# Where an arena in SBUF begins: 32 instead of 64 bytes beyond a multiple of 128

## The reference, cut to what matters

```
h = rms_norm(x);  proj = h @ w_in
x = x + merged(attention, rwkv, short conv; gates) @ w_out
x = x + square(relu(rms_norm(x) @ w_up)) @ w_down
```

```
u = causal_dwconv(h @ ffn_w_up);  y = (silu(gate) * val) @ ffn_w_down
x = layer_norm(DN_ALPHA * x + (1 + gate2) * y)
```

## Time and profile before

| | |
|---|---|
| median of 3 runs | 2519.72 us (2514.77 to 2530.96) |
| span of the profiled execution | 2510.8 us |
| the profiled execution's time around its span | not listed |
| mean granted TensorE clock | 0.974 |
| PE matmul busy | 2344.0 us, 93% |
| PE weight load busy | 2234.5 us, 89% |
| VectorE busy | 1948.0 us, 78% |
| ScalarE busy | 1391.5 us, 55% |
| GpSimd busy | 12.8 us, 1% |
| the 16 DMA engines | 49.9% |

### The profile page before, as it was taken

One profiled execution on the slowest core, in us unless ns is written; L12 is line 12 of the kernel. 1 busy time (PEld: TensorE's weight loads), 2 busy tenths in 40 slices (PEclk: granted clock), 3 DMA queues, 4 the chain that ended last, 5 costly groups with the idle time before them and its releaser, 6 DMA issues. The chain is left out here.

```text
span 2510.8 us, 45734 instructions
## 1 busy us (share of the span) xinstructions
PE 2344.0 (93%) x18552; PEld 2234.5 (89%) x18552; DVE 1948.0 (78%) x3439; ACT 1391.5 (55%) x2552; POOL 12.8 (1%) x20
## 2 busy tenths in 40 slices
PE   8899999989999998979998989999988999988998
PEld 7899999978898998879998879998788999867998
DVE  6578798856687986978897868886559889867885
ACT  7635565465365644746645657646554674533764
POOL 0000000000000000000000000000000000000000
PEclk9999999999999999999999999999989999989999
DMA  6215578723164776214575615583424458722552
GB/s 248 89 51 203 184 278 301 311 84 118 51 252 185 286 305 249 101 66 153 188 301 217 235 68 185 191 312 119 176 92 185 163 191 312 273 103 74 195 195 92
DMA packets 64225, 463.36 MB, mean 185 GB/s; under 512 B 7248, under 2 KB 7440, under 8 KB 8208
## 3 DMA queue, kind: packets, MB, share of 16 engines
q1 hardware_dynamic: 64016, 460.44, 49.4%
HBM read 459.37 MB, written 1.05 MB: 183 GB/s over the span
## 5 line engine op out<-in xcount | busy, mean ns | idle before, releaser
L730 PE MATMUL psum<-arena_rounded,upper_rounded 128*128 128x256 f32 (+2 forms) x5112 | 1439.8, 282 | 87.9 <-DVE ring_rounded L571 19.1
L731 PE MATMUL psum<-arena_rounded,upper_rounded 128*128 128x256 f32 (+2 forms) x5112 | 1426.6, 279 | 0.0
L732 PE MATMUL psum<-arena_rounded,ring_rounded 128*128 128x256 f32 (+2 forms) x5112 | 1426.0, 279 | 0.0
L730 PEld LDWEIGHTS psum<-arena_rounded,upper_rounded 128*128 128x128 f32 (+2 forms) x5112 | 969.6, 190 | 109.6 <-issue 69.2
L562 ACT ACTIVATE upper_rounded<-ring 128x1024 fp32r<-128x1024 f32 (+4 forms) x958 | 751.6, 796 | 521.6 <-PE psum L732 426.9
L571 DVE TENSOR_TENSOR ring_rounded<-ring,upper_rounded 128x1024 fp32r<-128x1024 f32 (+4 forms) x958 | 838.8, 897 | 259.3 <-ACT upper_rounded L562 254.4
L731 PEld LDWEIGHTS psum<-arena_rounded,upper_rounded 128*128 128x128 f32 (+2 forms) x5112 | 968.7, 189 | 0.7 <-issue 0.5
L732 PEld LDWEIGHTS psum<-arena_rounded,ring_rounded 128*128 128x128 f32 (+2 forms) x5112 | 969.0, 190 | 0.1
L586 DVE CUSTOM_DVE_ANT_0 ring<-ring,silu_c,cols 128x1024 f32<-128x1024 f32 x192 | 244.7, 1279 | 0.0
L2366 DVE SCALAR_TENSOR_TENSOR arena<-psum,cols,arena 128x255 f32<-128x255 f32 (+1 forms) x352 | 153.2, 477 | 56.8 <-ACT arena L2333 53.7
L2333 ACT ACTIVATE arena<-psum,cols 128x256 f32<-128x256 f32 x176 | 89.5, 561 | 72.9 <-PE psum L732 72.9
(11 more groups left out here) (497 smaller groups left out, 2348.8 us busy)
## 6 DMA issues: line engine op xcount, KB each, us to landing
ring<-stream_dram SPq DMA_DIRECT2D x434, 1024.0 KB, 4.9
const<-const_dram SPq DMA_DIRECT2D x1, 1540.0 KB, 14.6
x<-x_dram SPq DMA_DIRECT2D x1, 1024.0 KB, 4.8
out_dram<-x SPq DMA_DIRECT2D x4, 256.0 KB, 2.0
cols<-cols_dram SPq DMA_DIRECT2D x1, 974.0 KB, 11.3
silu_c<-c_dram SPq DMA_DIRECT2D x1, 512.0 KB, 15.3
const<-const_dram SPq DMA_DIRECT2D x1, 67.0 KB, 4.6
pos<-positions_dram SPq DMA_DIRECT2D x1, 64.0 KB, 5.7
```

Source lines behind the costliest of these rows:

```text
L730: pe.matmul(out, upper, x[0][:, b.k, :], start=(b.k == 0), stop=False)
L731: pe.matmul(out, upper, x[1][:, b.k, :], start=False, stop=False)
L732: ins = pe.matmul(out, lower, x[0][:, b.k, :], start=False, stop=(b.k == nk - 1))
```

## The change

The rest that the arena's beginning is asked to have goes from 64 to 32. As the tensors before it end at byte 112,416, which is 878 x 128 + 32, the gap of 8 floats (32 bytes) is no longer allocated and the arena begins at 112,416 instead of 112,448. Every tile in it, rounded or not, moves down by 32 bytes. Nothing else moves, and no instruction is added, removed or reordered.

```diff
         self.cos, self.pos = sb("cos", T), sb("pos", T, I32)
-        begin_at_multiple_of(128, 64)
+        begin_at_multiple_of(128, 32)
         self.arena = sb_rounded_too("arena", ARENA, ARENA_CUTS)
```

## The result

The changed kernel takes 2554.47 us in the median of 4 runs (2547.19 to 2558.15), the kernel before on the same chip 2520.8. The ratio is 1.0132, with a 95% interval of 1.0099 to 1.0166: slower, by some 33 us. The profiled execution took 2557.54 us, its span is 2555.7; the span before was 2510.8, so 44.9 us lie between the two profiles.

The account below looks back on a forecast made before the run. The prediction took TensorE's matmul spacing as the bound; terms 0 + 0 + 1 + 8 = +9 us on the median of 2519.7 gave 2529 us, with 2505 to 2577 us as the range for 8 in 10.

Parts of the forecast that it names:

- likeliest case: Split products keep their paces with at most some ns more or a few more slow stretches: 2529 us, chance 0.40.
- the prediction's own sign: The forecast is wrong if the share of slow stretches or a new pace moves the time by over 25 us.
- rival A: In dense stretches of split products the slow pace, 117.8 ns, becomes the rule: up to +57 us; chance 0.35.
- Steps 1 and 2: VectorE and ScalarE instructions on the arena: both taken as 0, bounds -8 to +8 us and +-3 us.
- Step 3: Plain 32-bit matmuls on TensorE, some 2,700 records: taken as +1 us, bounds +-2.7 us.
- Step 4: Split products on TensorE: 0.5 ns more for each of 15,504, +8 us, bounds -16 to +57 us.
- Rivals B: In stretches of split products the slow pace vanishes, all at 113.1 ns: 2505 us; chance 0.06.
- C: In dense stretches of split products a pace below 113.1 ns appears: -50 us, 2470 us; chance 0.07.
- D: Nothing changes at all, the paces of the split products stay: 2520 us; chance 0.12.
- The two other ways for step 4, to 0: For split products, independent read ports or 16-byte SBUF lines make the 32-byte move cost 0 instead of +8 us.

Follow-up runs that it names:

- e4: Against the kernel before, ring and rounded copy of the weights moved to rest 32 of 128, arena at rest 64 as before; ratio 1.01.
- e5: Against the kernel before, the arena alone moved up by 128 bytes, to rest 192 of 256; ratio 1.0136.
- e11: Against the kernel before, arena at rest 32 of 128 and both homes of the weights at rest 96, distance 192; ratio 0.9997.
- e12: Against the kernel before, arena at rest 0 of 128 and both homes of the weights at rest 64, distance 192; ratio 0.9988.
- e1: Against the kernel before, the arena alone moved to rest 0 of 128, weights at 0; ratio 1.0242.
- e10: Against the kernel before, the arena alone moved up by 384 bytes; ratio 1.0132.
- e6: Against the kernel before, all arena tiles moved up by 16 bytes, to rest 80 of 128, weights at 0; ratio 1.022.
- e2: Against the kernel before, the arena alone moved to rest 96 of 128, weights at 0; ratio 1.0163.
- e8: Against the kernel before, arena at rest 96 of 128 and rounded copy of the weights at 32, ring left at 0; ratio 1.0165.
- e9: Against the kernel before, the arena alone moved up by 256 bytes; ratio 1.0.
- e3: Against the kernel before, arena moved to rest 96 of 128, ring and rounded copy of the weights to rest 32; ratio 1.0096.

## Why the prediction was right or wrong

The time, 2554 us, lies in the range of 2505 to 2577, and the sign was that of the forecast. The size was not: 2529 us was forecast, +9 us, and +33 us came. In the chances the case that came, slower by over 1%, had 0.34, within 1% had 0.59. The likeliest case's own range, 2515 to 2543, was missed, and by the prediction's own sign (a new pace that moves the time by over 25 us) its forecast was wrong. The wide range holds the result because it was drawn up to rival A's end, not because the working behind 2529 was right.

**Steps 1 and 2** (VectorE, ScalarE: 0) were right, by the rows above: 418, 383 and 385 ns as before, and busy times within 1 us of 1948.0 and 1391.5.

**Step 3** (plain matmuls, +1 us) was right as to addresses: medians of 379 and 378 ns, unchanged. Their time still fell, for another reason, given below.

**Step 4** was the term that was mis-sized. It had 0.5 ns for each of 15,504 split products, +8 us. In the two traces PE is busy 1839.0 and 1896.1 us with the 15,624 split products that move 256 columns (each counted to the next start at most): +57.1 us, 3.7 ns for each; the mean spacing in gapless stretches rose by 3.8 ns. The step took the row of matmuls with both operands in `const` as the nearest, because their beginnings have rest 32. The experiments show that this was the wrong likeness: the rest of a single operand does not decide (e4 against e5; e11 and e12 against the changed kernel and e1), the distance of the two does, and plain 32-bit matmuls show no effect in their durations, neither at distance 0 (line 776) nor with a moving operand at each multiple of 4 bytes (line 2538). No row of the kernel before could show a split product at another distance; the only sign that something like it existed were the two paces in one trace.

**Rival A** said where and roughly how much, and missed the form. It expected the share of stretches at 117.8 ns to grow, with +25 us from 44% of them on. That does happen, but at distance 64 (e5, e10: +13 in a thousand), where the arena moves by 128 or 384 bytes. At 160, the changed kernel's, both old paces are gone, and the new ones are 117.33 and 118.67 ns. The window it named as its own sign, 917 matmuls in 108 us, looks much the same: the first of them, 1158 to 1266, has 919. Its counter-argument, that with one arrangement both paces occur and so addresses don't decide alone, was true and led astray: at one distance a stretch can take either pace, but which paces there are to take goes with the distance. **Rivals B, C and D** did not come. C was out in another sense: in fourteen arrangements none went below 113.33 ns in a long stretch.

**The two other ways for step 4, to 0,** both failed. With the arena at the same byte, weights 32 bytes lower (e5 against e4) turned 116.67 and 117.78 ns into 113.33 and 117.78; so what the Trainium skill, page "TensorE: Matmul & The Clock Gate", section "Step-by-step: what each phase is for", says of two independent read ports does not make the pace free of where the stationary operand lies here. The lines of 16 bytes of the Trainium skill, page "SBUF — State Buffer", section "Door 1: The DMA port swizzle (why `[64,N]` ≈ `[32,N]`)", don't bound the effect either: a move by one such line, e6, gave +2.2%.

**What reached the end.** The split products cost +57.1 us of PE's busy time, all other matmuls -7.6 us (505.0 to 497.4): 49.5 us. With 4.6 us less idle time the span grew by 44.9. That the others took less isn't an effect of addresses on them, as their medians stayed; fewer of their records fell into half clock: of line 2213's 128 records 8 took over 500 ns before and 1 after, of line 2538's 186 it was 17 and 6, and the mean granted clock was 0.974 and 0.976. The medians are 33.7 us apart and not 44.9, because the two profiled executions lie on opposite sides of theirs. That of after took 3.1 us more than its median. For that of before only the span is listed, 2510.8; the time of the other runs is 1.9 us above their span, so I estimate 2512.7 us, 8.1 below its median and below each of its four runs. (The prediction set its span directly against the median of times and got 8.9 us.) In later comparisons the median of before lay between 2511 and 2523 us, its runs between 2503 and 2533.

That scatter is part of the picture, and its cause is not shown. Kernels with one pace in their long stretches lie within 2.4 to 9.0 us (e2, e1, e8, e6, 4 runs each), kernels at distance 192, with two paces 4.4 ns apart, within 16 to 24 us (before, e11, e12, e9, with 4, 10, 10 and 12 runs). A changing share of slow stretches would do that, but no kernel was profiled twice, and the granted clock varies too: in e9 the fastest run, 2502.95 us, had 0.979 and the slowest, 2526.91 us, 0.970, while in e1 and e2 it lay within 0.002. How much of the 24 us is pace and how much clock, these runs don't separate.

Three things stay open. The runs show that the relation of the two operands' addresses sets the pace, and they don't show where in the chip the reads meet; and they show that a stretch mostly keeps the pace it restarted with, without saying what chooses it. It is not quite as the prediction had it, that the pace stays until a gap breaks it: in e3 a stretch without idle time goes at 113.33 ns from 218 us until 237.5 us and at 117.78 ns from there on, and in the kernel before one goes from the slow to the fast pace near 589 us, both at the full clock. And of the distances only 64 and 192 were run in more than one kernel; that 0, 32, 160, 176, 208 and 224 have the paces of the table rests on one profile each, and 96 (for all three products) and 128 were not run.

## What to carry to other kernels

When a kernel lives on back-to-back split products of 256 columns, the addresses of moving and stationary operand relative to each other are a tuning parameter worth up to 2.4% of this kernel: read the spacing (window length by count, where PE has no idle time), try the distances modulo 256, and fix the best one in the allocation, as any tensor that grows ahead of it changes it. Tune the distance and not one tensor's rest. And where runs on one core scatter by 1%, look at the granted clock and at the durations, stretch by stretch, before averaging more runs: one engine can have two paces at the same clock.

## What the runs showed of the hardware that was not expected

- Rounded 32-bit matmuls of 128 x 256 with a weight load each, at 2.4 GHz, go at one of 113.33, 116.67, 117.33, 117.78, 118.33, 118.67, 119.17, 119.26 or 120.00 ns in long stretches, and which of them occur goes with the distance of the operands' addresses modulo 256 bytes (the same pair in four kernels at 192 and in three at 64, one kernel each at the others). Distance 192 has the best mean (114.2 to 115.0 ns in four kernels), 0 the worst of those run (119.9 ns).
- 16 bytes to either side of it cost more than 32: 119.1 and 119.3 ns at 208 and 176, against 118.3 and 118.1 at 224 and 160.
- Distances 64 and 192 have the same two paces and a different share of them: means of 117.0, 116.8 and 117.6 ns against 114.3, 115.0, 114.2 and 114.7.
- Plain 32-bit matmuls, VectorE and ScalarE showed no effect of beginnings at multiples of 32 bytes above 1 ns, 4 ns and 2 ns (groups of lines 776, 2213 and 2538; 2378, 2135 and 2493; 2120 and 766).
